# Dense products of a hybrid decoder trunk: the three precision passes outside the column chunks

## The reference

```python
def even_mixer(x, ...):
    p = rmsnorm(x, g_norm) @ w_in            # q, k, v, gate, low rank, S5 input
    ...                                      # GLA heads and S5 groups
    return concat([o, z]) @ w_out
def odd_mixer(x, ...):
    p = rmsnorm(x, g_norm) @ w_in            # GeLU gate branch, conv + RG-LRU branch
    ...
    return (gate * h) @ w_out
def channel_mixer(x, g_norm, w_up, w_down):
    return square(relu(rmsnorm(x, g_norm) @ w_up)) @ w_down
for layer in range(2):
    x = x + mixer(x)                         # even, then odd
    x = x + channel_mixer(x)                 # 1024 -> 4096 -> 1024
y = rmsnorm(x)
```

## Time and profile before

| | us |
|---|---|
| median of 3 runs | 2533.03 |
| lowest and highest of them | 2528.7, 2535.57 |
| the profiled execution | 2526.41 |
| its span, from first to last instruction | 2524.3 |
| TensorE matmul busy in it | 2363.6 |
| TensorE weight load busy | 2275.7 |
| VectorE busy | 1224.8 |
| ScalarE busy | 635.2 |

### The profile page before, as it was taken

How to read it: one execution, slowest core, us unless ns; L and a number is a source line. 1 busy time by engine, 2 the same in 40 slices (tenths; PEclk the granted TensorE clock), 3 DMA queues, 4 the chain that set the end, 5 groups by cost and what they waited for, 6 DMA issues and landing times.

```text
span 2524.3 us, 32646 instructions
## 1 busy us (share of the span) xinstructions
PE 2363.6 (94%) x13974; PEld 2275.7 (90%) x13974; DVE 1224.8 (49%) x1333; ACT 635.2 (25%) x720; POOL 203.2 (8%) x113
## 2 busy tenths in 40 slices
PE   5867798798999999999999999999999999999996
PEld 4856687687999999999999988899999999999995
DVE  5995315633344344444443776654344434444444
ACT  5112122213241111212111455443221111121113
POOL 3830132200200000000000000000000000000003
PEclk8877789657999999999999999999999999999998
DMA  3214221103111111111111111111111111111111
GB/s 135 78 35 115 84 69 60 59 18 122 52 50 45 54 42 50 42 42 50 50 44 48 42 40 47 36 47 42 42 50 50 42 50 42 50 42 42 50 34 69
DMA packets 69209, 136.14 MB, mean 54 GB/s; under 512 B 24448, under 2 KB 40464, under 8 KB 69136
## 3 DMA queue, kind: packets, MB, share of 16 engines
q1 hardware_dynamic: 63808, 120.96, 14.8%
q0 software_dynamic: 2880, 10.49, 1.2%
q10 hardware_dynamic: 2448, 3.64, 0.4%
HBM read 119.17 MB, written 14.71 MB: 53 GB/s over the span
## 4 chain that ended last, share of the span: by engine, by line
PE 85%; DVE 9%; ACT 3%; issue 2%; DMA 0%; POOL 0%; ACTq 0%; POOLq 0%; DVEq 0%; SPq 0%
PE acc L547 78%; DVE TT L1409 3%; PE acc L775 2%; PE ms L672 1%; PE ms L670 1%; DVE XL L1409 1%; PE acc L786 1%; ACT TT L1110 1%; PE acc L790 1%; ACT L1110 0%; DVE XP L1409 0%; PE acc L798 0%; DVE X L1412 0%; DVE PT L1412 0%; DMA X<-in_x_t 0%
## 5 line engine op out<-in xcount | busy, mean ns | idle before, releaser
L547 PE MATMUL acc<-XH,WH 128*128 128x352 f32 x2664 | 870.0, 327 | 24.0 <-ACT TT L1110 14.1
L547 PE MATMUL acc<-XL,WH 128*128 128x352 f32 x2664 | 860.9, 323 | 0.0
L547 PE MATMUL acc<-XH,WL 128*128 128x352 f32 x2664 | 860.4, 323 | 0.0
L1409 DVE TENSOR_TENSOR X<-X,acc 128x1056 f32<-128x1056 f32 (+1 forms) x288 | 343.4, 1193 | 417.4 <-PE acc L547 404.2
L547 PEld LDWEIGHTS acc<-XH,WH 128*128 128x128 f32 x2664 | 506.3, 190 | 32.3 <-issue 27.7
L547 PEld LDWEIGHTS acc<-XL,WH 128*128 128x128 f32 x2664 | 507.3, 190 | 0.1
L547 PEld LDWEIGHTS acc<-XH,WL 128*128 128x128 f32 x2664 | 505.1, 190 | 0.0
L547 PE MATMUL acc<-HH,WH 128*128 128x352 f32 x1536 | 498.0, 324 | 2.1 <-DVE X L1409 2.1
L547 PE MATMUL acc<-HL,WH 128*128 128x352 f32 x1536 | 493.4, 321 | 0.0
L547 PE MATMUL acc<-HH,WL 128*128 128x352 f32 x1536 | 493.1, 321 | 0.0
L1008 ACT ACTIVATE WH<-WR 128x1024 fp32r<-128x1024 f32 x152 | 156.5, 1049 | 598.2 <-PE acc L547 538.7
(11 more groups left out here) (297 smaller groups left out, 1635.4 us busy)
## 6 DMA issues: line engine op xcount, KB each, us to landing
WR<-in_w_stream SPq DMA_DIRECT2D x159, 512.0 KB, 3.2
WR<-in_w_stream POOLq DMA_DIRECT2D x20, 512.0 KB, 3.9
X<-in_x_t SPq DMA_DIRECT2D x3, 1408.0 KB, 12.1
TT<-z_scratch SPq DMA_DIRECT2D x8, 528.0 KB, 3.4
X<-in_x_t SPq DMA_DIRECT2D x8, 528.0 KB, 7.1
out_y_t<-X SPq DMA_DIRECT2D x12, 352.0 KB, 2.4
u_scratch<-UR SPq DMA_DIRECT2D x4, 576.0 KB, 3.1
U<-u_scratch SPq DMA_DIRECT2D x32, 72.0 KB, 2.6
```

What stands on the lines that cost most here:

```text
L547: ins = pe.matmul(out, lhs, rhs, start=start, stop=stop)
L1409: return dve.tensor_tensor(out, a, b, op)
```

## The change

In `product` the two inner loops change places: the passes become the outer loop and the chunks the inner one. For each k the nine matmuls are the same; their order changes from chunk 0 (three passes), chunk 1 (three passes), chunk 2 (three passes) to pass 0 (three chunks), pass 1 (three chunks), pass 2 (three chunks). `start` and `stop` are still set on the first and last pass of each bank.

```diff
@@ -564,8 +564,8 @@
                     if xn is not None and (ks[0] == 0 or k < ks[0]):
                         pe.wait_ge(xl_done, xn + k + 1)
                     s, col = slots(k), cols(k)
-                    for c in range(NCH):
-                        for i, (w, x) in enumerate(PASSES):
+                    for i, (w, x) in enumerate(PASSES):
+                        for c in range(NCH):
                             last = mm(acc[:, t % 2, c, 0:CH], w[:, s, col:col + P],
                                       ops[x](k)[:, cols_of(c)], k == ks[0] and i == 0, k == ks[-1] and i == 2)
                     if free and k != ks[-1]:
```

## The result

The changed kernel is slower: a median of 2558.69 us (2556.58 to 2562.91, 4 runs) against 2531.18 us before (2528.7 to 2535.57, 4 runs). The ratio is 1.0113 with a 95% interval of 1.0096 to 1.013, that is 24 to 33 us. The forecast was 2533 us and no change, with 2522 to 2542 as its range. The profiled execution took 2562.91 us, its span 2560.7. One run of a later kernel (`chunks_outermost`) took 4581.72 us in place of some 2528 for a reason that isn't known, and no ratio uses it.

A forecast was written before the change was run, and what follows sets the result against it. The prediction took TensorE's dense matmuls, their number times the distance between two starts, to bound the kernel. Its terms, 0 + 0 + 0 + 0 us, left the median like the one before: 2533 us, range 2522 to 2542.

The forecast's parts named there:

- What bounds the kernel: Whole kernel: TensorE, busy 94% of the span; dense products take the matmul count times the distance between starts, 158.9 ns.
- Removed: nothing: Weight loads in the whole kernel: a repeated tile is still loaded, the count stays at 13,974; 0 us.
- Steps with an unchanged weight tile: 0 us: In `product`, 5,472 more steps keep their weight tile; loads lie beside other work; 0 us, bounds 66.8 us gain, 16.4 us loss.
- The straight line: Fit through 352- and 512-column matmul steps: 0.456 ns a column, -1.6 ns at zero columns, so nothing fixed per matmul.
- Bank changes: 0 us: In `product`, 8,208 more PSUM bank changes taken as free; 0 us, with ends of -14.0 and +24.6 us.
- rival C: Slower: in `product` a bank change costs something hidden; at 3 ns each, 2558 us. Chance 0.04.
- a count below 3766: Sign for the slower, bank-change rival: fewer than 3766 matmuls in the 600 us stretch (0.3%).
- Order within a tile: 0 us: Signals and waits in `product` keep their places and causes, no wait added and no DMA moved; 0 us.
- A: Faster: a repeated tile makes the load cheap, and the load holds the stream back; 2466 us. Chance 0.03.
- B: Faster: rotating over banks frees a stream held back by accumulating again into the same bank; 2383 us. Chance 0.03.
- D: Granted clock: a shift in its rise or fall moves the time either way. Chance 0.01 on either side.
- What the change does to the steps: List for `product`: 8,208 more bank changes and 5,472 more steps with an unchanged weight tile.

The follow-up runs named there:

- `chunks_outermost`: Kernel before with the chunk as outermost loop where no wait stands inside the product, so a bank is kept for all k: 2528.07 us, ratio 1.0005.
- `weights_of_after`: Kernel before with weight tiles in the changed kernel's order (WH six times, WL three), moving slices and banks as before: 2524.79 us, ratio 1.0002.
- `one_weight_tile`: Kernel before with all nine matmuls of a k on tile WH, moving slices and banks as before: 2526.84 us, ratio 1.0002.
- `banks_of_after`: Kernel before, operands in its own order, but the bank changes at every matmul as in the changed kernel: 2527.2 us, ratio 0.9998.
- `banks_of_before`: Changed kernel's operand order, but banks in the order of the kernel before, three matmuls in a row to each: 2555.96 us, ratio 1.0117.
- `passes_outside_starts_of_before`: Changed kernel's loops, slices beginning at columns 320c, 32 more in pass 1, giving the earlier sequence of starts modulo 256 bytes: 2526.78 us, ratio 1.0005.
- `weights_shifted`: Loops of the kernel before, all moving slices begun on the same 256-byte multiple, plus the weight tile's start moved 128 bytes: 2521.78 us, ratio 0.9971.

## Why the prediction was wrong, step by step

**What bounds the kernel.** Right. The time after is the count of dense matmuls times the distance of two starts, and the 2.9 ns by which the distance grew account for the difference of the spans.

**Removed: nothing.** Right: 13,974 loads before and after.

**Steps with an unchanged weight tile: 0 us.** The term was right (`weights_of_after` 1.0002, `one_weight_tile` 1.0002). The main reason given for it was not, so that the right value was in part luck: "Nothing fixed is paid per matmul; the excess grows with the columns, so it belongs to the stream". The straight line joined 352-column matmuls with the 512-column ones of `values`, which have other tensors as tile and slice and other starts. Nor did the other argument hold, that the step to the same tile would be shorter if the load had a share, "Both are 0.16 us": the view rounds to 10 ns, and below that the steps differ. By the starts in the trace the mean is 160.9 ns to the same tile, 158.3 to a new tile and 157.5 to a new bank, and kernels with other tiles and banks at these places have the same steps, so the differences aren't theirs. With one thing changed at a time the excess is the same 13.3 ns at 352 and at 384 columns.

**Bank changes: 0 us.** The term was right (`banks_of_after` 0.9998 with nine changes in nine), and rival C, which put a price on it, was wrong. C named 2558 us, and 2558.7 was measured, but the mechanism isn't there: its 3 ns came from the recorded length of XH,WH, and `banks_of_before` loses as much without the extra bank changes. Its sign, a count below 3766, was met as well (3709). A rival's number that fits proves nothing of its cause, and this sign would have been met by any slower step.

**Order within a tile: 0 us.** Right as to signals and waits; the waits after are those of before.

**Rivals A, B and D.** None came about: no kernel with more repeats or with banks in rotation was faster, and the granted clock was full in the dense stretch, where the loss is seen.

**The step that failed** is the list in "What the change does to the steps". It counted bank changes and unchanged weight tiles, and left out the third thing that the swap of the loops changes, the start of the moving slice. The order of the slices costs 3.0 ns on each of the 12,312 matmuls, 36 us by the profiles and 24 to 33 us by the runs, and no term of the sum stood for it. All other terms were zero and stayed zero, so the chance of 0.88 rested on a list that wasn't complete. The forecast of "steps of 0.15 to 0.17 us whatever the pair" held in the view and hid a spread from 155.1 to 161.5 ns before and 158.2 to 167.6 after. A sign was in view: XH,WH lasted 323 ns against 321 and 320, which I tried to pin on the bank and on the weight tile. It belongs to the pattern of the slices too. In `passes_outside_starts_of_before`, where each pair stands at all three places of a run, the difference is gone (groups of line, stretch 800 to 1400):

```profile
L547 PE MATMUL acc<-XH,WL 128*128 128x352 f32 x624 | 133.0, 321 | 0.0
L547 PE MATMUL acc<-XH,WH 128*128 128x352 f32 x624 | 133.0, 321 | 0.0
L547 PE MATMUL acc<-XL,WH 128*128 128x352 f32 x624 | 132.9, 321 | 0.0
```

**What stays open.** Shown is that, with the weight tiles where they are, the loss comes from the sequence of the starts of the moving slices, even and odd; that the start of the weight tile shifts the pace; and that banks, repeats of the tile, contiguity and the choice of XH or XL don't. Not shown is what resource stream and load share, whether the length of the load or the number of output rows made the narrow tiles faster, why one sequence costs more than another, and why one can have two paces (161.7 and 158.3 ns). A conflict in the memory that both read would fit, but it was only argued. All starts tried are multiples of 128 bytes. `weights_shifted` is faster than the kernel before by 0.3% but multiplies wrong weights; a full computation with all slices even and all tiles odd would need padded slices and wasn't built.

## What to carry to other kernels

When a loop swap leaves every count the same, list all that changes between neighbours on the engine, the start address of each operand included, before calling the swap free; here it was worth 1.1% with not one wait or load more. A fixed cost per matmul should be read from two widths of the same operands, not from two different products. And to find a cause of a few nanoseconds per instruction, permute one property at a time, with no regard to the result of the computation, and read the count of instructions in a stretch without idle time: 3778 against 3709 decides where medians that scatter by 0.3% don't. Where even single steps are in question, look first at how far the view rounds.

## What was unexpected of the hardware

- In a stream of fp32r matmuls of 352 columns at the full granted clock, the distance of two starts was 158.3, 158.9, 159.4, 160.0, 161.7 or 161.9 ns, with no instruction added, depending on whether moving slices begin, counted from their tensor, on a multiple of 256 bytes or 128 bytes past it, in what sequence, and on which of the two the weight tiles begin.
- One sequence, the strictly alternating one, ran at 161.7 ns in one stretch and at 158.3 ns in another of the same execution, and its runs fell into two groups 13 us apart.
- Moving the weight tile's start by 128 bytes changed the distance from 160.0 to 158.3 ns; halving its columns, and with them the output rows, to 157.7.
- Single steps of one stream differed by up to 9 ns (158.2 to 167.6) in a cycle that repeats. Kernels with the same sequence of starts had the same cycle, whatever their tiles and banks.
- Changing the PSUM bank at every accumulating matmul cost nothing (3778 matmuls in 600 us either way).
